# Fourteen pairs of each FFN up projection as seven half products a pair (one level of Strassen's scheme)

## The reference

```python
def conv_ffn(x, w_up, conv_w, conv_b, w_down):      # x: 512 x 1024, w_up: 1024 x 5632, w_down: 2816 x 1024
    h = x @ w_up
    h = causal depthwise convolution of width 3 along the tokens, + conv_b
    gate, val = jnp.split(h, 2, axis=-1)
    return (jax.nn.silu(gate) * val) @ w_down
```

## Time and profile before

| | us |
|---|---|
| median of 3 runs | 2069.28 (2067.76 to 2073.63) |
| the profiled execution | 2073.53 |
| its span | 2071.8 |

### The profile page before, as it was taken

How to read it: one execution, slowest core, us unless ns; L and a number is a source line. 1 busy time by engine, 2 the same in 40 slices (tenths; PEclk the granted TensorE clock), 3 DMA queues, 4 the chain that set the end, 5 groups by cost and what they waited for, 6 DMA issues and landing times.

```text
span 2071.8 us, 32448 instructions
## 1 busy us (share of the span) xinstructions
PE 2053.4 (99%) x11724; PEld 1728.4 (83%) x11724; DVE 1413.2 (68%) x2250; ACT 1023.9 (49%) x1671; POOL 398.3 (19%) x454
## 2 busy tenths in 40 slices
PE   9999999999999999999999999999999999999998
PEld 8889888888988888888877898888878889888886
DVE  5665555999366555699788655456987666554897
ACT  4754333557334433456556644334565764333555
POOL 0520211310000121120045401212200520121220
PEclk9999999999999999999999999999999999999999
DMA  8123322384430332267421113233674131233383
GB/s 287 63 102 102 100 88 95 120 262 157 143 132 31 102 101 92 90 189 244 156 72 42 62 41 104 99 101 96 193 229 163 63 103 60 87 98 101 105 265 117
DMA packets 73881, 251.62 MB, mean 121 GB/s; under 512 B 8448, under 2 KB 12672, under 8 KB 73392
## 3 DMA queue, kind: packets, MB, share of 16 engines
q1 hardware_dynamic: 58752, 213.10, 31.2%
q0 software_dynamic: 7168, 16.78, 3.7%
q10 hardware_dynamic: 7856, 20.34, 2.8%
HBM read 248.04 MB, written 6.34 MB: 123 GB/s over the span
## 4 chain that ended last, share of the span: by engine, by line
PE 85%; DVE 9%; ACT 2%; DMA 2%; issue 1%; POOL 0%; DVEq 0%; ACTq 0%; SPq 0%; POOLq 0%
PE ps L2011 16%; PE ps L2013 16%; PE ps L2012 16%; PE ps L2196 6%; PE ps L2530 4%; PE ps L2532 4%; PE ps L2531 4%; PE ps L2083 2%; DMA raw<-slabs 2%; DVE w_lo L1352 2%; PE ps L2039 2%; PE ps L2041 2%; PE ps L2040 2%; PE ps L2071 1%; PE ps L2055 1%; PE ps L2056 1%
## 5 line engine op out<-in xcount | busy, mean ns | idle before, releaser
L2011 PE MATMUL ps<-h_hi,w_hi 128*128 128x512 f32 (+1 forms) x1552 | 606.6, 391 | 0.0
L2012 PE MATMUL ps<-h_lo,w_hi 128*128 128x512 f32 (+1 forms) x1552 | 603.2, 389 | 0.0
L2013 PE MATMUL ps<-h_hi,w_lo 128*128 128x512 f32 (+1 forms) x1552 | 603.2, 389 | 0.0
L1747 DVE SCALAR_TENSOR_TENSOR work<-ps,conv_sb,work 128x511 f32<-128x511 f32 (+1 forms) x352 | 246.2, 744 | 379.4 <-ACT work L1138 379.2
L1352 DVE TENSOR_TENSOR w_lo<-raw,w_hi 128x1024 fp32r<-128x1024 f32 x356 | 439.1, 1240 | 43.6 <-ACT w_hi L777 39.9
L777 ACT ACTIVATE w_hi<-raw 128x1024 fp32r<-128x1024 f32 x368 | 384.5, 1051 | 129.9 <-DVE raw L1836 71.8
L1138 ACT ACTIVATE work<-ps,conv_sb 128x512 f32<-128x512 f32 x176 | 137.0, 778 | 474.7 <-PE ps L2013 445.5
L2011 PEld LDWEIGHTS ps<-h_hi,w_hi 128*128 128x128 f32 x1552 | 291.4, 188 | 62.6 <-issue 4.0
L2013 PEld LDWEIGHTS ps<-h_hi,w_lo 128*128 128x128 f32 x1552 | 291.3, 188 | 60.5
L2012 PEld LDWEIGHTS ps<-h_lo,w_hi 128*128 128x128 f32 x1552 | 291.5, 188 | 58.6
L718 POOL TENSOR_TENSOR bias<-act 128x256 f32<-128x256 f32 x40 | 78.7, 1967 | 996.4 <-DVE act L1753 996.4
(11 more groups left out here) (289 smaller groups left out, 3367.5 us busy)
## 6 DMA issues: line engine op xcount, KB each, us to landing
raw<-slabs SPq DMA_DIRECT2D x368, 512.0 KB, 3.8
act<-slabs POOLq DMA_DIRECT2D x64, 256.0 KB, 5.5
bias<-slabs SPq DMA_DIRECT2D x16, 512.0 KB, 6.1
act<-slabs SPq DMA_DIRECT2D x12, 512.0 KB, 5.7
bias_dram<-bias_rows ACTq DMA_DIRECT2D x2, 2048.0 KB, 13.3
g_post<-gains ACTq DMA_DIRECT2D x8, 512.0 KB, 4.9
bias<-bias_dram ACTq DMA_DIRECT2D x2, 2048.0 KB, 9.6
g_pre<-gains ACTq DMA_DIRECT2D x7, 512.0 KB, 6.9
```

Of the source, the lines that this page charges most:

```text
L1747: ve.scalar_tensor_tensor(y, ps[:, 2 * par + e, 0:SEQ - sh], conv_sb[:, L, t, tap:tap + 1], y, ALU.mult, ALU.add).then_inc(done, 1)
L2011: pe.matmul(ps[:, bank, cols], hi, h_hi[:, k, cols], start=k == 0, stop=False)
L2012: pe.matmul(ps[:, bank, cols], hi, h_lo[:, k, cols], start=False, stop=False)
L2013: last = pe.matmul(ps[:, bank, cols], lo, h_hi[:, k, cols], start=False, stop=k == KT - 1)
```

## The change

Pairs 4 to 17 (`FAST`, `FAST_END`) of each layer leave the loop. A pair's two slabs are taken as a 2 x 2 matrix: rows are value (the odd slab, `row1`, quarters a11 and a12) and gate (the even one, `row2`), columns are the first and last four of the eight blocks. h is a 2 x 2 matrix too: channel halves by token halves of 256. Seven products of 4 x 3 matmuls of 256 columns take the place of 2 x 8 x 3 of 512.

- **Weight sums.** x1 = the gate slab's two halves added, by a DMA that adds one half from DRAM onto the other in `raw`; x2 = x1 + a11 on DVE; x3 = a11 + the gate slab's first half, by an adding DMA from DRAM; x4 = a12 + x2, by an adding DMA from `raw` to `raw`. The sign of the gate row is turned, which `conv_neg` takes back in the taps. x1 with a22 behind it is split as one slab of 1024 elements, a11 with a12 as another; x2, x3 and x4 are 512 each.
- **h sums**, once a layer: DVE joins the parts of h into `vbuf` (four quarters of 4 x 256), forms four differences, ACT and DVE split them into `g_post`/`g_pre`, `work` and `x`. So x is stored in DRAM as the stage begins (`x_out`, four DMAs on ACT's queue) and reloaded behind pair 18 (`x_back`).
- **C sums.** Three copies of a partial sum on ACT (`copy`, into the free part of `bias`), three adds in PSUM on DVE (`c11`, `c22`, `c12`).
- **Order.** `period(q)` on ACT and DVE carries pair q's products and pair q - 1's rest. POOL's `down_sums` are cut in halves, one to a period, behind the DMAs of x3 and x4.

The code on each engine, cut:

```diff
+FAST, FAST_END = 4, 18
 # SP
+for q in range(FAST, FAST_END):
+    even = up_slab(L, q + 2)
+    sp.wait_ge(x4_in[q % 2], sum_count(L, q))
+    sp.wait_ge(up_lo, 3 * fast(L, q) + 3)
+    sp.dma_start(raw[:, raw_slot(even), :], slabs[dram(even)]).then_inc(raw_in[raw_slot(even)], 16)
+    ring(even + 1)
 # POOL
+def x1(q):
+    pool.wait_ge(raw_in[slot], raw_count(even))
+    pool.dma_start(raw[:, slot, 0:SEQ], slabs[dram(even)][:, SEQ:D], accum_op=ALU.add).then_inc(x1_in[q % 2], 16)
+def x3_x4(q):
+    pool.wait_ge(up_x2, fast(L, q) + 1)
+    pool.dma_start(raw[:, row1, 0:SEQ], slabs[dram(even)][:, 0:SEQ], accum_op=ALU.add).then_inc(x3_in[q % 2], 16)
+    pool.dma_start(raw[:, row1, SEQ:D], raw[:, row2, 0:SEQ], accum_op=ALU.add).then_inc(x4_in[q % 2], 16)
+for q in range(FAST, FAST_END):
+    x3_x4(q)
+    if q > FAST:
+        down_sums(L, halves // 2, halves % 2)
+        halves += 1
+    if q + 2 < FAST_END:
+        x1(q + 2)
 # ACT, part_hi
+if name == "x1":
+    sc.wait_ge(x1_in[q % 2], sum_count(L, q))
+    sc.wait_ge(w_used, up_slab(L, q - 2) + (1 if q >= FAST + 2 else 2))
+    s = 1 + 2 * (q % 2)
+    sc.activation(w_hi[:, s, :], raw[:, row2, :], ACT.Copy).then_inc(up_hi, 1)
 # DVE, period
+if q > FAST + 1:
+    fast_taps(q - 2, 1)
+    gate((q - 2) % 2, (q - 2) // 2)
+if q > FAST:
+    c11(q - 1)
+if q + 1 < FAST_END:
+    part_lo(q + 1, "x1")
+if q > FAST:
+    c22(q - 1)
+if q + 1 < FAST_END:
+    part_lo(q + 1, "a11")
+    x2(q + 1)
+part_lo(q, "x3")
+part_lo(q, "x4")
+if q + 1 == FAST_END:
+    split_lo(up_slab(L, q + 1))
+    split_lo(up_slab(L, q + 1, 1))
+if q > FAST:
+    fast_taps(q - 1, 0)
+if q + 1 < FAST_END:
+    part_lo(q + 1, "x2")
+if q > FAST:
+    c12(q - 1)
 # PE
+def p4(q):
+    pe.wait_ge(up_copy, 3 * fast(L, q) + 3)
+    pe.wait_ge(in_lo, 4 * L + 4)
+    product(q, 0, 0, "a22", in_parts(3), False, True).then_inc(w_used, 1)
+def p3(q):
+    pe.wait_ge(up_c, 3 * fast(L, q) + 2)
+    pe.wait_ge(lo_made, made(up_slab(L, q, 1)))
+    product(q, 1, 1, "x4", h_quarter(1, 1), False, True).then_inc(w_used, 1)
+def p7(q):
+    pe.wait_ge(up_copy, 3 * fast(L, q) + 2)
+    pe.wait_ge(lo_made, made(up_slab(L, q)))
+    product(q, 0, 0, "x3", in_parts(1), False, True).then_inc(up_mm, 1)
+for q in range(FAST, FAST_END):
+    p1_p2(q)
+    if q > FAST:
+        p4(q - 1)
+    p6_p5(q)
+    if q > FAST:
+        p3(q - 1)
+    p7(q)
+pe.wait_ge(tap0, UP_SLABS * L + 2 * FAST_END - 2)
+forward(n, 0, 0, range(0, 3))
+p4(FAST_END - 1)
+forward(n, 0, 0, range(3, 7))
+p3(FAST_END - 1)
+forward(n, 0, 0, range(7, KT))
```

More of the change, by code:

```diff
@@ L1152, in pair @@
                     split_hi(n0 + 2 * c + 1 + AHEAD, i)
+                for t in range(TT):
+                    sc.wait_ge(xn_made, TT * (2 * L + 1) + t + 1)
+                    sc.dma_start(x_dram[t], x[:, t, :]).then_inc(x_out, 16)
                 end = FFT // 2 - 1
[L1155 to L1159, removed]
+                pair(0)
+                pair(1)
+                for n in range(4):
+                    in_high(n)
+                tap(0, 1, 0)
+                tap(0, 1, 1)
+                part_hi(FAST, "x1")
+                silu(0, 1)
+                part_hi(FAST, "a11")
+                tap(1, 1, 0)
+                part_hi(FAST, "x2")
+                tap(1, 1, 1)
+                silu(1, 1)
+                for q in range(FAST, FAST_END):
+                    period(q)
+                q = FAST_END - 1
+                copy(q, 2)
+                fast_tap(q, 0)
+                split_hi(up_slab(L, q + 2))
+                silu(q % 2, q // 2)
+                split_hi(up_slab(L, q + 2, 1))
+                fast_tap(q, 1)
                 pair(0, end - 1)
+                sc.wait_ge(w_used, up_slab(L, FAST_END))
+                for t in range(TT):
+                    sc.dma_start(x[:, t, :], x_dram[t]).then_inc(x_back, 16)
                 operand(L, 0)
@@ L1373, in y @@
                         ve.wait_ge(x_new, p0 + t)
+                    elif k > 0 and k % 2 == 0:
+                        ve.wait_ge(x_back, 8 * TT * k)
                     ve.wait_ge(post_r, p0 + t + 1)
@@ L1760, in pair @@
                     split_lo(n0 + 2 * c + 1 + AHEAD, i)
+                if L == 0:
+                    ve.wait_ge(consts_in, 16 * EXTRA)
+                    ve.tensor_scalar(conv_neg[:, :, :, :], conv_sb.rearrange("p l (q e) f -> p l q e f", e=2)[
+                        :, :, FAST:FAST_END, 0, 0:3], -1.0, None, ALU.mult).then_inc(neg_made, 1)
                 end = FFT // 2 - 1
[L1763 to L1767, removed]
+                for n in range(4):
+                    join(n)
+                pair(0)
+                differ(0)
+                differ(1)
+                pair(1)
+                differ(2)
+                differ(3)
+                in_low(0)
+                in_low(1)
+                in_low(2)
+                taps(0, 1)
+                part_lo(FAST, "x1")
+                gate(0, 1)
+                part_lo(FAST, "a11")
+                x2(FAST)
+                in_low(3)
+                part_lo(FAST, "x2")
+                taps(1, 1)
+                gate(1, 1)
+                for q in range(FAST, FAST_END):
+                    period(q)
+                q = FAST_END - 1
+                fast_taps(q - 1, 1)
+                gate((q - 1) % 2, (q - 1) // 2)
+                c11(q)
+                c22(q)
+                split_lo(up_slab(L, q + 2))
+                fast_taps(q, 0)
+                split_lo(up_slab(L, q + 2, 1))
+                c12(q)
+                fast_taps(q, 1)
+                gate(q % 2, q // 2)
                 pair(0, end - 1)
@@ L2516, in pair, with product @@
                     forward(n0 + 2 * c + 1, i, 2 * par + 1)
-                with pe.Fori(1, FFT // 2) as i:
-                    for c in range(2):
-                        pair(c, i)
+                def product(q, e, half, name, operand, begin, onto=False):
+                    o = ps[:, up_bank(q, e), HALF * half:HALF * (half + 1)]
+                    (hi, lo), (b_hi, b_lo) = up_parts(q, name), operand
+                    for k in range(KT // 2):
+                        w = slice(k * P, (k + 1) * P)
+                        pe.matmul(o, hi[:, w], b_hi[:, k, :], start=begin and k == 0, stop=False, skip_group_check=onto)
+                        pe.matmul(o, hi[:, w], b_lo[:, k, :], start=False, stop=False, skip_group_check=onto)
+                        last = pe.matmul(o, lo[:, w], b_hi[:, k, :], start=False, stop=k == KT // 2 - 1, skip_group_check=onto)
+                    return last
@@ L2523, in ffn_down @@
+                n = up_slab(L, FAST_END)
+                pe.wait_ge(tap0, UP_SLABS * L + 2 * FAST_END - 2)
[4 more added lines that the diff above has]
+                forward(n, 0, 0, range(7, KT))
+                forward(n + 1, 0, 1)
+                for c in range(FAST_END + 1, FFT):
+                    pair(c % 2, c // 2)
             def ffn_down(L, k):
```

222 lines of the change are left out of this document (215 added, 7 removed).

## The result

The changed kernel takes 2167.74 us (median of 4 runs, 2165.66 to 2170.51), the kernel before 2071.45 beside it (2067.76 to 2076.08): ratio 1.0464, 95% interval [1.0436, 1.0492]. It is 96 us slower, where 59 were forecast. The profiled execution has a span of 2168.8 us.

The account below looks back on a forecast made before the run. PE's pace bounds the kernel before; after the change a PE-ACT-DVE loop, 11.4 us a period against 10.88. Twelve periods (136.8) plus ends make 167.1 a layer against 152.3: +59 us, 2133 (2128 on the median), range 2102 to 2170.

Parts of the forecast that it names:

- The cut and its limit: PE, pairs 4 to 17: seven products of 1.44 us, 10.08 against 10.88 a pair; at most 45 us saved, 2.2%.
- The loop that I find: Loop over PE, ACT and DVE through L1270 and p7: period 11.4 us; PE waits 1.3 us ahead of every p7.
- rival 1: The DMA loop binds, at 12.1 us a period: +34 us, 2162; chance 0.17, with port blocking.
- the second path: From x3 low over c12 to p4: 4.4 us, PE there after 4.55; binds if ACT or DVE is 0.2 late.
- the path over p7: Chain of p7, p1, p2, p4, then ACT's x1 and DVE's steps to x3 low: sums to 11.39 us a period.
- The DMA loop: x2 sum, x3/x4 issue, landing, slab load, x1 landing, over two periods: 21.4 us, 10.7 a period, under 11.4.
- Edits at nothing: Storing and reloading x, POOL's halved sums, PE's unrolled stream: no cost; without cover, x up to 12 us a layer.
- Ends of the stage: Entry 2.9 us lost at p7 of pair 4, x1 for pair 6 1.0 late; exit period 17 takes 15.7, not 10.08.
- The stall before pair 18: PE, each layer: one wait of some 5 us ahead of pair 18's forward product, in a period of 15.7 us.
- The port: DVE and POOL delaying each other: 0 in the sum, up to 0.4 x 48 = 20 us for the range.
- rival 2: The array stays the bound and the kernel is faster: 141.1 against 152.3 a layer, -45 us, 2024; chance 0.06.
- rival 3: Array-bound, but the ends stay: 151.3 us a layer, -4 us, no change; chance 0.03.

Follow-up runs that it names:

- run 7: Changed kernel with x4 added by POOL itself in place of the adding DMA: 2314.77 us, ratio 1.1166 to the kernel before, period 14.09 us.
- run 11: Changed kernel with x4 added on POOL, x3 parts first on ACT and DVE, POOL's half sums behind its last pair: one execution, 2176.94 us, period 11.34 us.
- run 2: Changed kernel with ACT and DVE taking pair q's x3 parts ahead of pair q+1's a11 parts and x2 sum: 2168.78 us, ratio 1.0470 to the kernel before.
- run 4: Changed kernel with the reload of x issued in the down projection, not at the start of the last four pairs: 2149.17 us, ratio 1.0375 to the kernel before.
- run 9: Run 4 plus, in the last period, pair 18's slabs split behind ACT's other work and DVE's taps of pair 16: 2142.12 us, ratio 1.0331.
- run 6: Changed kernel with x4's DMA issued ahead of x3's and the x3 parts first on ACT and DVE: 2198.92 us, ratio 1.0600 to the kernel before.
- run 8: Changed kernel with x4 added on POOL and the x3 parts first on ACT and DVE: 2237.72 us, ratio 1.0795 to the kernel before, period 12.65 us.
- run 10: Changed kernel with POOL issuing x3, x1, x4 in that order, plus the edits of run 4 and run 9: 2201.41 us, ratio 1.0620 to the kernel before.
- run 1: Changed kernel with x3 and x4 of pair q+1 issued ahead of x1 of q+2 in POOL's queue: 2275.41 us, ratio 1.0977 to the kernel before.
- run 5: Changed kernel with POOL's order of run 1, but the down pairs' half sums behind x1: 2274.88 us, ratio 1.0975 to the kernel before.

## Why the prediction was right, and where not

**Direction and range** held: slower, and 2167.7 lies inside 2102 to 2170, though at its end. The forecast of +59 us fell short by 37.

**The cut and its limit held.** 256 columns run at 0.120 us in the products too, and seven products at 1.44 are less than a pair before. The saving was lost in the period, as said: 11.57 us are 0.69 over the 10.88 of the earlier trace rows.

**"The loop that I find": place right, releaser wrong.** PE idles ahead of p7 for DVE's low part of x3. For L1270 I wrote that PE releases it and named "L1270 waiting for DMA" as the sign of rival 1; that sign is what the trace shows, 41 times of 56. PE's wait there is 0.85 us, not 1.3. So in the steady part the case that came is a form of rival 1, at 11.57 instead of 12.1, and that the period came out within 0.2 us of the one reckoned for another loop is luck. The engine loop is real but by these runs shorter than 11.4 (both are estimates): about 11.2 in the order of the change (run 7 less its stretch), about 11.0 with the x3 parts first (run 11 less its own). In both runs it is the second path, over c12 and p4; the path over p7 that gave 11.39 is in the chain for no more than three periods in any run.

**The step that failed: "The DMA loop".** I drew it through two periods and got 10.7 a period. Its times were fair: landings of 5.7 to 6.5 for x3 and x4, 4.9 for x1, loads of 3.5. But I left out the order of POOL's queue. x1 of pair q+2 waits there for a load that waits for x4 of q, and x3 and x4 of q+1, whose x2 sum is done 2.5 us before (271.89 against 274.38 for x3's issue), stand behind it. That closes the loop within one period: 1.12 + 6.42 + 3.60 + 0.3 = 11.44. (Two of its sums are off, and nothing rests on them: by its terms every minimum gives 8.5, not 8.7, and every maximum 14.2, not 13.9.) Its price over the forecast is small, 48 x 0.17 = 8 us. That it is ring R which binds rests on the chains of the change and of runs 2, 4 and 9 (42 to 44 of 48 periods each) and on the step from run 2 to 11; no run shortened R alone, since each order tried closed a longer ring, and x4 on POOL brought in the port. Of the five orders of POOL's queue that ran, the given one was the fastest (that of run 6 was tried with the x3 parts first alone).

**"Edits at nothing": the mis-sized term.** The prediction let the x transfers cost nothing and named the end of the range: up to 12 us a layer without cover. The store is indeed free (in layer 0 pair 4 starts at 206.20, where it started at 206.08). The reload is not: run 4 gives back 18.6 us in four layers, 15 of them in the down projections, of the 37 that were missing. I looked at the mean share of the DMA engines, 30%, and at ACT's need for x, not at who else waits for a load just then. All of the growth of the down projection, 25 us, lies outside the stage that I costed. 18 of them are longer waits of PE and 7 its half clock behind them. Run 4 gives 15 back; the other 10 stay, 8 of them as waits: its trace shows 11.5 us of waits against 3.5 before. Beside the 0.9 in each layer there is one of 1.7, for a slab's low part, near the end of the down projection in three of them.

**Ends of the stage.** Entry: x3's low part of pair 4 was forecast for 214.6, and p7 starts at 214.36. The stall before pair 18 was forecast as one long period; it came as 2.15 + 2.97 us. Together the stretch up to the down projection took 72 us over before, against 59: 8 from the period and some 5 from the exit, by difference. The prediction has no term for TensorE's clock, and this is where it is missing: behind the two waits PE runs at half clock in all four layers, and the longer steps of its matmuls add up to 6.6 us.

**The port.** Reckoned at 0 with 20 us for the range. In the change POOL's sums fall beside taps, and the medians of DVE's subtractions are their minima (L2007: 0.684 and 0.682 us): 0 was right. Runs 7 and 8, and in part 6 and 10, show that it was right only because of the place.

**Rivals 2 and 3** fell: PE's slack never came, and even run 11, without any DMA in the chain, has a period of 11.34, over the 10.88 to beat.

## What to carry to other kernels

Draw the loops of a software pipeline through the queues too: an instruction that waits at the head of a queue lends its wait to all behind it, and an order that looks like an improvement for one operand can close a ring of one period where there had been two. Price a transfer by what is in flight beside it and by what waits for those others, not by the mean load of the DMA engines. When a loop is bound several ways within a few per cent, taking time out of one path can give nothing, and only a run tells which path is next.

## What the hardware showed that was not expected

- **A DMA's landing goes by what is in flight beside it.** Adding DMAs of 256 KB, medians. Alone: 4.0 us (x1, runs 7, 8 and 11). Beside slab loads of 512 KB, the first issued 0.3 us behind it: 5.7 (x3, runs 8 and 11). In bursts of three beside such a load: x1 4.9 issued first, 7.0 second (run 10) and 7.6 third (run 5); x3 5.7 second and 7.4 third (run 6). The place in the burst and the moment at which the load starts changed together, and no run parts them.
- **One row of POOL operations blocks one DVE subtraction for as long as it lasts**: 4.21 us for 0.69 beside four of them, 1.06 beside a single one of 1.60 (run 11). It ends 0.55 us behind the row's last operation in both.
- **The granted clock can halve at a stop of TensorE, and does not at every one.** In run 1 it is 1.00 up to the last matmul before a stop of 2.58 us, and then (windows of run 1) 0.50, that is 1.2 of 2.4 GHz:

```profile
262.00:265.10 3.10, 3.10 (x27) 2.93 (x25) 0.21 (x1) 0.10 (x1) 0.00 (x0) 1.00 0.80 192
267.70:270.80 3.10, 3.08 (x14) 3.09 (x15) 3.07 (x5) 1.91 (x4) 0.99 (x2) 0.50 0.00 0
```

  The length of the stop alone does not tell. The exit of layer 0 has the same two waits in the change (2.15 and 2.97 us) and in run 4 (2.15 and 2.96), and these are the windows behind them, first the change, then run 4:

```profile
372.70:375.90 3.20, 3.20 (x10) 2.55 (x9) 0.30 (x1) 0.00 (x0) 0.00 (x0) 0.50 0.00 0
372.70:375.90 3.20, 3.20 (x21) 2.86 (x20) 0.38 (x2) 0.00 (x0) 0.00 (x0) 1.00 0.00 0
```

  A stop of 1.84 us was followed by 0.50 (run 6), one of 3.26 us was not (run 5).

  At the tail of the change it costs, on top of the 5.05 us, about 9 matmuls x 0.2 = 1.8 us in layer 0, and at the exit 1.7, so these waits are dearer than their length. Behind the waits of 0.85 us ahead of p7 the matmuls keep their 0.120 us.
